# Hybrid decoder layer, opening: order of the third tile's differences, three portions of gate products, and the queue of the gate weights' load

## What is computed

```python
def hybrid_layer(h, norm_w, w_in, conv_w, ...):
    u = rmsnorm(h, norm_w)
    proj = jnp.einsum('btd,dc->btc', u, w_in)
    hg_q, hg_f, hg_i, hg_z, gd_qkv, gd_z, gd_a, gd_b = jnp.split(proj, cuts, axis=-1)
    ...
    g = -jnp.exp(gdn_A_log) * jax.nn.softplus(gd_a + gdn_dt_bias)
    beta = jax.nn.sigmoid(gd_b)
```

## Time and profile before

| | |
|---|---|
| median of three runs | 692.07 us (691.67 to 693.25) |
| the profiled execution: its time | 692.72 us |
| its span, first to last instruction | 690.9 us |
| what lies around the span | 1.8 us |
| granted TensorE clock, mean | 0.995 |
| PE busy | 673.3 us (97%) |
| DVE, POOL, ACT busy | 413.5, 375.8, 324.2 us (60, 54, 47%) |

### The profile page before, as it was taken

The page is one execution under the profiler, slowest core; times in us unless marked ns, Lnnn a source line. Parts: engine busy times, 40 slices in busy tenths (PEclk is TensorE's granted clock), DMA queues, the critical chain, the costliest instruction groups (busy, mean ns, idle before and its releaser), DMA issues. The chain is left out here.

```text
span 690.9 us, 13130 instructions
## 1 busy us (share of the span) xinstructions
PE 673.3 (97%) x4585; PEld 640.8 (93%) x4585; DVE 413.5 (60%) x977; ACT 324.2 (47%) x918; POOL 375.8 (54%) x581
## 2 busy tenths in 40 slices
PE   6999999999999999999999999999999999999995
PEld 4799999989999999999999999999999998888884
DVE  7836446278882472597933634888426257866256
ACT  7545432746654416466445254555452354242333
POOL 4547342268773343587824343887442559866324
PEclk9999999999999999999999999999999999999998
DMA  8744334221214347532548332023254325212014
GB/s 277 72 45 83 31 35 84 27 32 32 42 34 62 51 74 37 24 24 37 39 57 72 70 43 31 2 39 51 55 85 145 90 64 189 85 55 84 1 61 183
DMA packets 64004, 44.96 MB, mean 65 GB/s; under 512 B 17446, under 2 KB 59044, under 8 KB 63940
## 3 DMA queue, kind: packets, MB, share of 16 engines
q1 hardware_dynamic: 63764, 43.81, 36.0%
q10 hardware_dynamic: 176, 0.33, 0.1%
HBM read 35.88 MB, written 7.65 MB: 63 GB/s over the span
## 5 line engine op out<-in xcount | busy, mean ns | idle before, releaser
L283 PE MATMUL proj<-uTh,w_high 128*128 128x352 f32 (+4 forms) x768 | 262.0, 341 | 0.0
L283 PE MATMUL proj<-uTh,w_low 128*128 128x352 f32 (+4 forms) x768 | 245.7, 320 | 0.0
L283 PE MATMUL proj<-uTl,w_high 128*128 128x352 f32 (+4 forms) x768 | 245.2, 319 | 0.0
L283 PEld LDWEIGHTS proj<-uTh,w_high 128*128 128x128 f32 x768 | 145.1, 189 | 0.2
L283 PEld LDWEIGHTS proj<-uTl,w_high 128*128 128x128 f32 x768 | 145.1, 189 | 0.0
L283 PEld LDWEIGHTS proj<-uTh,w_low 128*128 128x128 f32 x768 | 144.3, 188 | 0.0
L326 POOL TENSOR_TENSOR w_low<-w_raw,w_high 128x256 fp32r<-128x256 f32 (+1 forms) x54 | 76.1, 1420 | 47.2 <-DVE decay L379 26.8
L1356 POOL TENSOR_TENSOR level_k<-hg_k,f_suffix 128x64 f32<-128x64 f32 (+1 forms) x144 | 64.4, 467 | 10.5 <-PE mix L1827 5.0
L1366 POOL TENSOR_TENSOR f_suffix<-f_suffix,f_prefix 128x192 f32<-128x192 f32 x84 | 52.3, 622 | 17.8 <-DVE f_prefix L1621 6.0
L1668 DVE SCALAR_TENSOR_TENSOR conv_out<-conv_in,hg_taps,conv_out 128x352 f32<-128x352 f32 (+2 forms) x81 | 55.2, 681 | 0.0
L1621 DVE TENSOR_TENSOR f_prefix<-f_prefix 128x192 f32<-128x192 f32 x84 | 43.9, 523 | 13.9 <-POOL f_suffix L1366 13.1
(11 more groups left out here) (331 smaller groups left out, 1416.3 us busy)
## 6 DMA issues: line engine op xcount, KB each, us to landing
w_raw<-in_w_in SPq DMA_DIRECT2D x32, 512.0 KB, 8.5
x_tile<-in_x SPq DMA_DIRECT2D x8, 512.0 KB, 8.5
w_raw<-y_scratch SPq DMA_DIRECT2D x8, 384.0 KB, 4.4
decay<-gamma_scratch SPq DMA_DIRECT2D x4, 576.0 KB, 3.7
landing<-in_w_out SPq DMA_DIRECT2D x4, 512.0 KB, 7.8
landing<-in_x SPq DMA_DIRECT2D x3, 512.0 KB, 8.3
out_y<-landing SPq DMA_DIRECT2D x3, 512.0 KB, 2.6
y_scratch<-gd_y SPq DMA_DIRECT2D x6, 192.0 KB, 2.6
```

The source lines that it names most:

```text
L283: last = pe.matmul(acc[:, 0:tw], w[j % 2][:, k, :], u[:, k, t0:t0 + tw], start=(k == 0 and i == 0), stop=(k == KT - 1 and i == 2))
```

## The change

- The load of the gate weights goes from SP's list (between tiles 4 and 5) to ACT's, behind `norm_raw`. It is then issued at the very beginning, on another queue than the tiles.
- ACT makes `gate_h` one round earlier: behind `high_part(1)` and `square_tile(4)`, ahead of `high_part(2)`.
- `gate_l` goes from DVE to POOL, behind `rstd_tile(4)`.
- DVE takes `low_part(3)` ahead of `scale_tile(4)` instead of behind it.
- PE makes the gate products of the first piece in three portions, 4, 6 and 6 products behind tiles 3, 4 and 5, instead of 8 and 8 behind tiles 4 and 5.

```diff
@@ sync
             load_x(i)
-        sp.dma_start(gate_raw[:, :, :], w_in_v[:, :, AB_COLS:AB_COLS + 2 * HEADS]).then_inc(gate_in, 16)
         load_x(5)
@@ gpsimd
         for i in range(NC):
             rstd_tile(i)
+            if i == 4:
+                pool.wait_ge(gate_high, 1)
+                pool.tensor_tensor(gate_l, gate_raw[:, :, :], gate_h.bitcast(F32), ALU.subtract).then_inc(gate_low, 1)
             if i >= NC - 3 and i < NC - 1:
                 first_split(i - NC + 3)
@@ scalar
         act.dma_start(nraw[:, :], norm_w[0:1, :].broadcast_to([META, D])).then_inc(nrow_in, 16)
+        act.dma_start(gate_raw[:, :, :], w_in_v[:, :, AB_COLS:AB_COLS + 2 * HEADS]).then_inc(gate_in, 16)
         for i in range(AHEAD):
             square_tile(i)
         for i in range(NC):
@@
                 square_tile(i + AHEAD)
-            if i == 2:
+            if i == 1:
                 act.wait_ge(gate_in, 16)
                 act.copy(gate_h, gate_raw[:, :, :]).then_inc(gate_high, 1)
@@ vector
         for i in range(NC):
-            if i + 1 < NC:
+            if i + 1 < NC and i != 3:
                 scale_tile(i + 1)
             for half in range(2):
                 low_part(i, half)
             if i == 3:
-                dve.wait_ge(gate_high, 1)
-                dve.tensor_tensor(gate_l, gate_raw[:, :, :], gate_h.bitcast(F32), ALU.subtract).then_inc(gate_low, 1)
+                scale_tile(i + 1)
@@ tensor
+        GATE_KS = {3: range(0, 2), 4: range(2, 5), 5: range(5, KT)}
         for i in range(NC):
@@
-            if i in (4, 5):
-                gate_piece(0, range(4 * (i - 4), 4 * (i - 4) + 4))
+            if i in GATE_KS:
+                gate_piece(0, GATE_KS[i])
```

## The result

The changed kernel takes 694.35 us (median of eight runs, 692.79 to 695.29), the kernel before beside it 691.87 us (691.47 to 693.30): 1.0030 times as long, 95% interval 1.0018 to 1.0042. Run again later (`after_again`) it came to 1.0024 (1.0015 to 1.0033). So it is slower by 2.5 us, the way that was forecast and within the range (692.2 to 698.2), and 1.5 us less than the 695.9 of the likeliest case. But it is slower for another reason than that case's: the profile shows nearly what the second rival said (the pieces get ahead of the first tiles), to which I had given 0.08. That the time fell into the range of a case that didn't happen is luck.

The account below looks back on a forecast made before the run. The prediction took TensorE as the bound from 17.5 us on, fed by tile loads, ACT and DVE. Later restart 2.5, transposes 0.9 and clock 0.4 made 3.8 us on 692.07: 695.9 us, range 692.2 to 698.2.

Parts of the forecast that it names:

- the likeliest case: Gate weights land late, at 16.0 us, and ACT, DVE and TensorE wait: 3.8 us slower, 695.9; chance 0.66.
- the second rival: Gate pieces run beside tile 1 ahead of the first tiles, delaying DVE: +1 to +2.5 us, 693.8; chance 0.08.
- The path: Opening: tile loads, ACT, DVE, TensorE; whatever tile 8's transposes, at 27.28 us, lose or win, the end does too.
- The landing of the gate weights: DMA queues take turns of one packet, so the gate weights land between 14.8 and 18.0 us; 16.0 taken.
- My test for it: Sign: ACT's gate copy waits some 4 us for a DMA; without that wait, turns aren't one piece each.
- the share of 0.35: DMA engines' busy share during the gate load before the change, against 1.01 while tiles stream; so most should hide.
- The eight transposes more: At TensorE's restart, tile 4's eight transposes are still to do: 0.9 us added.
- DVE's order: Low part of tile 3 first puts tile 4's scaling 1.21 us later; its transposes add 0.9 us at TensorE's restart.
- The clock: TensorE's longer idle stretch may lengthen its time at 1.2 GHz: 0 to 1.5 us lost, 0.4 taken.
- Neither POOL nor the issue on ACT: Gate difference on POOL lies beside ACT's work, and one more issue on ACT, 0.43 us: both cost nothing.
- In time, not slower: Gate weights land by 12.2 to 12.9 us, tiles keep pace: -0.4 to +0.7 us, middle 692.3; chance 0.22.
- The clock stays up: Three portions keep TensorE busy, saving its 3.42 us at 1.2 GHz: 691.4; chance 0.04, shared with anything unseen.

Follow-up runs that it names:

- queue_only: The kernel before with only the load of the gate weights moved to ACT's queue, all orders as before: 1.0011 times the kernel before.
- order_only: The changed kernel with the gate load back at its old place on SP's queue, orders, portions and POOL as changed: 1.0001 times the kernel before.
- few_pieces: The changed kernel with the gate load's same 32 KB in 128 pieces instead of 1024: 0.9995 times the kernel before.
- sp_second: The changed kernel with the gate load on SP's queue again, directly behind tile 1: 1.0034 times the kernel before.
- dve_order_back: The changed kernel with DVE's old order, scaling of tile 4 ahead of the low part of tile 3: 1.0051 times the kernel before.
- later_issue: The changed kernel with the gate load still on ACT's queue but issued behind the square of tile 0: 697.64 us, 1.0066 times the kernel before.
- gate_after6: The kernel before with the gate load behind tile 6 on SP's queue and ACT's gate copy one round later: 0.9990 times the kernel before.
- order_again: The same program as order_only, run on another chip: 1.0006 times the kernel before.

## Why the prediction was right and wrong

**The path, right.** Over 14 profiles of this case, the first product behind tile 8's transposes and the end of the span keep their distance whatever the opening does:

```
                 first product      span    difference
before           28.07              690.9   662.8
after            28.81              691.4   662.6
after_again      29.39              692.0   662.6
queue_only       28.91              691.4   662.5
order_only       30.31              693.1   662.8
few_pieces       29.73              692.6   662.9
sp_second        31.27              694.4   663.1
dve_order_back   30.50              693.2   662.7
later_issue      33.12              695.8   662.7
gate_after6      27.40              690.1   662.7
```

That 662.5 to 663.1 us follow is the step on which every number rested, and it held. (The four left out give 662.5 to 662.8.) The medians don't follow the profiles to the tenth: the profiled execution of the changed kernel took 693.14, 1.2 us less than its median, that of the kernel before 692.72, 0.85 us more than its median.

**The landing of the gate weights, wrong; the step that failed.** "The gate weights land with tile 8, however early they are issued": they landed at 9.4, not at 16.0. The row of the two last stores showed two queues that were both full, and turns of one were the right reading of it, as `later_issue` shows. I carried it over to a place where I hadn't asked whether both queues would be full. My test for it was wrong too: "if it isn't there, turns aren't one piece each"; the wait wasn't there, and they are. The trace had a hint in the issues: behind `gate_raw` at 3.12 the next issue of SP, tile 5 at 3.60, took 1.84 us where the tiles ahead of it took 0.40 to 0.43. I didn't price it. And I misread: the share of 0.35 is that of 9.0 to 9.5 alone, the lowest of five half microseconds (0.58, 0.35, 0.69, 0.88 and 0.83 from 8.5 on), and it lies ahead of the stretch from 9.7 to 12.9 to which I put it.

**What took its place.** Tile 2 landed at 9.5 instead of 7.1. The second rival had this mechanism, pieces that get ahead of the first tiles, at 693.8; I argued it down with the earlier trace rows to 0.08. Its size was near (694.35), its place one tile further on: tile 1 was untouched (square at 5.51, before 5.63), though its issue began no earlier than that of the gate weights (1.27 against 1.25). In the two profiles with the queue alone it was at 5.90 and 6.27, so it isn't always spared, and what spares it no run shows.

**From the late tile to the end.** The restart came 0.7 us later (18.28 against 17.56), much less than the 2.4 us of tile 2, because tile 5 was no longer late, ACT's wait of 0.98 us had gone and DVE's difference of the gate weights too. The eight transposes more that I added for tile 4 were there, behind the first portion. In the first profile the end of the opening moved by only 28.81 - 28.07 = 0.7 us, because its clock stayed up while that of the kernel before had fallen for 3.4 us; in `after_again`, with the clock late, by 1.3 us against the first profile of before and 0.9 against the second. The medians differ by more, 2.5 and 1.7 us; that rest lies in executions that weren't profiled, and isn't explained.

**DVE's order, mis-priced.** I wrote that it delays tile 4's scaling and costs 0.9 us of transposes at the restart. True of the kernel with that order against the one before, but I didn't work out what the portion behind tile 3 would cost without it: 1.9 us, `dve_order_back`. With the load at its old place the orders together cost nothing that can be measured (1.0001, 1.0006), so the 0.9 us of that term is more than was found, too, though the second interval, up to 1.3 us, doesn't exclude it.

**The clock.** My term of 0.4 us, between 0 and 1.5, was to be a loss that adds itself. What the profiles show is a difference between executions of one kernel, 0.6 us between two of the changed one. It goes into the spread, and the changed kernel has no clear share of it. What the term reckoned with, a longer idle stretch followed by a longer time at 1.2 GHz, is there in other kernels: 6.8 us of it behind waits of 3.75 and 3.36 us (`order_only`, `order_again`), and up to 26.3 behind the 7.18 us of `later_issue`, against 3.4 us behind 1.03 in the earlier trace rows. The changed kernel's wait was only 1.45 us.

**Neither POOL nor the issue on ACT cost anything, right.** The difference on POOL took 0.31 us at 14.88, while TensorE's restart waited for the low part of tile 3 until 18.28. The first square began at 3.35 (3.38 before).

**The other rivals.** "In time, not slower" was right that the weights came in time (9.4, copy without a wait) and wrong that this settles it. "The clock stays up" did happen in the first profile and won nothing over the kernel before.

## What to carry to other kernels

In these runs a load of many tiny pieces cost the loads issued behind it, on whatever queue they were; to take it off one queue and issue it earlier on another can put it ahead of the very loads that the start depends on. Before moving a load, write down the order of issue over all queues, and ask which load comes next behind it and who waits for that one. If a portion of products is put behind an earlier step on TensorE, what it waits for must be moved forward with it, or all the work behind it stands.

## What the runs showed of the hardware

- The two queues of SP and ACT took turns of one packet each where both had pieces ready, whatever the size: 394 against 406 packets from 8 to 12 us in `later_issue`. 32 KB in 1024 pieces then landed 13.6 us behind their issue.
- They didn't where the small pieces were issued ahead of tile 2: 34 against 415 packets from 4.8 to 6.4 us, with the engines idle two thirds of the time.
- The same 32 KB in 128 pieces, at the same place, left tile 2's square at 7.89 instead of 9.52.
- The granted clock that the stretches show is 1.00 ahead of the trace's first record of it, and isn't to be believed there. Eight transposes took 1.97 us at 8.56 and, in the same profile at 21.00, 1.04 us, both in stretches that print 1.00 (and the slow products of `after_again` at 18.16 stand in such a stretch too, so that the mean granted clocks of two executions can't be compared by their last digits):

```profile
8.56:10.40 1.84, 1.84 (x8) 1.56 (x8) 0.60 (x1) 0.88 (x1) 0.00 (x0) 1.00 1.04 421
21.00:21.80 0.80, 0.80 (x11) 0.80 (x8) 0.80 (x2) 0.80 (x3) 0.40 (x1) 1.00 1.03 66
```

So TensorE's opening starts at the lower of the two levels, 1.2 GHz, in this profile as in that of the kernel before (1.91 us for the eight at 12.70), and the earlier trace rows doesn't show a fall from a clock that had been up all along, as I read it, but one short stretch at 2.4 GHz between two at 1.2.
